# A two-layer hybrid decoder on one core: memory pieces, masks and scores of three mixers put in other places

## The reference, cut to what matters

```python
for l in range(DEPTH):
    p = rmsnorm(x, norm_mix[l]) @ w_in[l]
    y_a = hgrn2_mixer(...)             # o = state part + masked scores @ v, norm, gate
    y_b = gated_deltanet_mixer(...)    # triangular solve per 64-token chunk
    y_c = rglru_mixer(...)             # a = exp(log_a); h_t = a h_(t-1) + u, times gelu(gate)
    y_d, v_first = rwkv7_mixer(...)    # decay, delta update, group norm, bonus
    x = x + concat([y_a, y_b, y_c, y_d]) @ w_out[l]
    k, v = mem_n @ xattn_wk[l], mem_n @ xattn_wv[l]     # depends on the memory alone
    x = x + attention(rmsnorm(x, norm_xattn[l]), k, v) @ xattn_wo[l]
    x = x + (swiglu if l == 0 else moe_swiglu)(rmsnorm(x, norm_ffn[l]))
```

## Time and profile before

| | |
|---|---|
| median of 3 runs | 1963.12 us (1962.64 to 1963.27) |
| the profiled execution | 1961.31 us, of which the span of the trace is 1959.5 |
| TensorE busy, granted clock | 95% of the span, 0.981 |
| VectorE, ScalarE busy | 75%, 57% |
| layer 0: mixers | about 114 to 290 us |
| layer 1: mixers | about 667 to 845 us |
| experts | from about 957 us to the end |

### The profile page before, as it was taken

How to read it: one execution, slowest core, us unless ns; L and a number is a source line. 1 busy time by engine, 2 the same in 40 slices (tenths; PEclk the granted TensorE clock), 3 DMA queues, 4 the chain that set the end, 5 groups by cost and what they waited for, 6 DMA issues and landing times.

```text
span 1959.5 us, 29713 instructions
## 1 busy us (share of the span) xinstructions
PE 1861.4 (95%) x12520; PEld 1605.6 (82%) x12521; DVE 1465.5 (75%) x1543; ACT 1121.3 (57%) x1057; POOL 0.2 (0%) x4
## 2 busy tenths in 40 slices
PE   7997899999999978999699999999999999999996
PEld 6986789899989866897588888888888888888884
DVE  6778645554467687453789989889899898998985
ACT  5563134434344641244567777677776777767774
POOL 0000000000000000000000000000000000000000
PEclk9998999999999989999899999999999999999998
DMA  7520234355555212243599999989999999999992
GB/s 243 172 75 15 66 108 165 108 181 185 194 157 164 89 45 66 74 164 111 184 393 342 373 330 384 370 335 371 337 383 365 335 372 348 369 364 339 369 373 97
DMA packets 239450, 465.99 MB, mean 238 GB/s; under 512 B 11856, under 2 KB 87760, under 8 KB 239312
## 3 DMA queue, kind: packets, MB, share of 16 engines
q1 hardware_dynamic: 239312, 464.03, 66.4%
HBM read 462.95 MB, written 1.05 MB: 237 GB/s over the span
## 4 chain that ended last, share of the span: by engine, by line
PE 88%; DVE 9%; issue 1%; ACT 1%; DMA 1%; DVEq 0%; SPq 0%; ACTq 0%
PE ps L2148 31%; PE ps L1617 16%; PE ps L2158 16%; PE ps L1602 12%; PE ps L1637 8%; DVE MT L907 2%; PE ps L2204 2%; PE ps L2179 1%; PE ps L1682 1%; PE ps L2219 1%; DVE MT L913 1%; DVE TMP L907 1%; DVE MT L910 1%; DMA raw<-in_w_in 1%; DVE spare_hi L907 0%
## 5 line engine op out<-in xcount | busy, mean ns | idle before, releaser
L1380 DVE TENSOR_TENSOR wlo<-raw,whi 128x2048 fp32r<-128x2048 f32 x140 | 320.5, 2292 | 55.7 <-ACT whi L787 55.4
L787 ACT ACTIVATE whi<-raw 128x2048 fp32r<-128x2048 f32 x140 | 268.9, 1922 | 121.1 <-PE ps L2158 71.3
L920 DVE TENSOR_TENSOR wlo<-raw,whi 128x2048 fp32r<-128x2048 f32 x85 | 194.6, 2289 | 85.3 <-ACT whi L480 85.1
L1380 DVE TENSOR_TENSOR wlo<-PT,whi 128x2048 fp32r<-128x2048 f32 x84 | 192.1, 2293 | 31.2 <-ACT whi L787 30.1
L480 ACT ACTIVATE whi<-raw 128x2048 fp32r<-128x2048 f32 x85 | 162.1, 1907 | 64.7 <-PE ps L1637 36.6
L2148 PE MATMUL ps<-whi,hE_hi 128*128 128x512 f32 x672 | 185.5, 398 | 2.4 <-DVE hE_lo L1449 2.4
L787 ACT ACTIVATE whi<-PT 128x2048 fp32r<-128x2048 f32 x84 | 161.5, 1922 | 34.9 <-PE ps L2148 34.2
L2148 PE MATMUL ps<-wlo,hE_hi 128*128 128x512 f32 x672 | 180.2, 390 | 0.0
L2148 PE MATMUL ps<-whi,hE_lo 128*128 128x512 f32 x672 | 179.9, 390 | 0.0
L2148 PEld LDWEIGHTS ps<-wlo,hE_hi 128*128 128x128 f32 x672 | 126.2, 188 | 27.1
L2148 PEld LDWEIGHTS ps<-whi,hE_lo 128*128 128x128 f32 x672 | 126.2, 188 | 26.5
(11 more groups left out here) (297 smaller groups left out, 3356.7 us busy)
## 6 DMA issues: line engine op xcount, KB each, us to landing
raw<-in_moe_w_up SPq DMA_DIRECT2D x111, 1024.0 KB, 7.0
PT<-in_moe_w_down SPq DMA_DIRECT2D x56, 1024.0 KB, 6.5
PT<-in_moe_w_gate SPq DMA_DIRECT2D x55, 1024.0 KB, 6.9
TMP<-in_moe_w_gate SPq DMA_DIRECT2D x55, 1024.0 KB, 6.8
raw<-in_moe_w_down SPq DMA_DIRECT2D x55, 1024.0 KB, 6.1
raw<-in_w_in SPq DMA_DIRECT2D x28, 1024.0 KB, 5.3
raw<-in_ffn_w_gate SPq DMA_DIRECT2D x11, 1024.0 KB, 5.3
raw<-in_ffn_w_up SPq DMA_DIRECT2D x11, 1024.0 KB, 5.7
```

Of the source, the lines that this page charges most:

```text
L787: nc.scalar.activation(ex_hi[m % XSPL], ex_raw[m % XRAW], ACT.Copy).then_inc(S("w_hi"), 1)
L920: V.tensor_tensor(wlo[i % SPL][:, :], raw[d % RAW][:, :], whi[i % SPL][:, :].bitcast(F32), ALU.subtract).then_inc(S("w_lo"), 1)
L1380: V.tensor_tensor(ex_lo[m % XSPL], ex_raw[m % XRAW], ex_hi[m % XSPL].bitcast(F32), ALU.subtract).then_inc(S("w_lo"), 1)
```

## The change

- The third mixer's first ten operations on VectorE go from the first mixer's levels 0 to 3 into the input projection (after chunks 9 to 11), one goes from level 4 to level 6, and its end goes from the second mixer's inverse to behind the fourth's.
- The fourth mixer's decay sums go from the second mixer's inverse to the input projection; its first scaling goes from VectorE to ScalarE.
- Of the fourth mixer's scores and masks, two score products go into the second mixer's tail and two into its own inverse; one mask stands before the second mixer's output, three are in the inverse, at levels 0, 3 and 5. That inverse keeps two slices of a piece, at level 0.
- The pieces are given out anew: in layer 0 eight, eight and one slice in the first mixer, 15 and more in the second, 16 behind the fourth's inverse. Layer 1's piece 0 goes around the feed-forward's norm and piece 1 around its own first norm. The loads follow.
- The first mixer's output goes to another bank and is copied to SBUF, and bank 7 is used for pieces alone.
- The parameters are loaded by ScalarE's queue, and constants of the decays of both layers are computed before the first statistics, with two table loads more there.

The diff, cut to what is spoken of:

```diff
+PIECES = [[("xattn_wk", j) for j in range(4)] + [("xattn_wv", j) for j in range(4)],
+      [("xattn_wv", 0)] + [("xattn_wk", j) for j in range(4)] + [("xattn_wv", j) for j in range(1, 4)]]
...
+kv = [[("kv", name, layer, CM_COLS * j) for name, j in PIECES[layer]] for layer in range(DEPTH)]
...
-    pieces = [("kv", name, layer, c) for name in ("xattn_wk", "xattn_wv") for c in range(0, D, CM_COLS)]
+    if layer:
+        out += kv[1][1:2]
...
-    out += pieces[0:4] + w_out[0:1] + pieces[4:6] + w_out[1:2] + pieces[6:7] + w_out[2:4] + pieces[7:8]
+    out += kv[layer][2 * layer:4 + layer] + w_out[0:1] + kv[layer][4 + layer:6] + w_out[1:2] + kv[layer][6:7] + w_out[2:4] + kv[layer][7:8]
...
+        out += kv[1][0:1]
...
-KV_BANK = [[7, 6, 7, 7, 7, 7, 2, 1], [7, 6, 7, 7, 7, 7, 2, 3]]
+KV_BANK = [[7, 6, 7, 7, 7, 1, 2, 1], [3, 1, 7, 7, 7, 7, 2, 3]]
...
+    if l and j == 1:
+        kv_put(1, 1)
...
-            kv_put(l, 0)
...
         if v == 3:
...
-            kv_put(l, 1)
+            if l == 0:
+                kv_put(0, 0)
         if v == 4:
...
-            kv_put(l, 2)
+        if v == 6:
+            kv_put(l, 1 + l)
...
-    a(tmp(5), ps[:, 7, :], ACT.Square).then_inc(S("o_sq"), 1)
...
+    a(tmp(5), ps[:, 6, :], ACT.Square)
+    a(h_out(l), ps[:, 6, :], ACT.Copy).then_inc(S("o_sq"), 1)
+    for c in range(2):
...
+        a(K_KK[:, s_], pt(D_K)[:, s_], ACT.Copy, scale=pc("rwkv_k_k", l, c))
...
 def deltanet(l):
+    kv_put(l, 2 + l)
     rwkv_ahead(l)
...
-    kv_put(l, 3)
+    kv_put(l, 3 + l)
...
     head_rms(l)
-    kv_put(l, 4)
+    kv_put(l, 4 + l)
...
 def rwkv(l):
...
-    kv_put(l, 5)
...
+        if l == 0 and t == 0:
+            kv_put(0, 5)
...
+        if j == 0:
+            kv_put(1, 0)
...
+act.dma_start(par[:, :], A["params"]).then_inc(S("par_in"), 16)
+table("exp_and_others")
...
+for k in range(DEPTH):
...
+    a(col(lam[k], 2), par[:, o2:o2 + 2], ACT.Abs)
+    a(col(expa[k], 4), par[:, o:o + 4], ACT.Exp)
+    a(col(lam[k], 2), col(lam[k], 2), ACT.Exp, scale=-1.0)
+table("natural_log")
+for k in range(DEPTH):
+    a(col(lam[k], 2), col(lam[k], 2), ACT.Ln, bias=1.0).then_inc(S("softplus"), 1)
...
+        rglru(l, -4)
     if j == 10:
+        rglru(l, -3)
...
+    if j == 11:
+        rglru(l, -2)
...
+        ts(pt(C_X), pt(C_X), -float(np.exp(-0.5)), ALU.mult)
+        for i in range(4):
...
+            chain.link(lambda: V.tensor_tensor_scan(K_B[:, s_], ones, pt(C_X)[:, s_], 0.0, ALU.mult, ALU.add))
+        ts(col(ST_NC0, 4).unsqueeze(2), many(K_B)[:, :, HD - 1:HD], -1.0, ALU.mult)
...
-            tt(col(lam[k], 2), col(lam[k], 2), col(lam[k] + 2, 2), ALU.add)
-            ts(col(lam[k], 2), col(lam[k], 2), -16.0, ALU.mult)
 def rglru(l, v):
-    la, ex = H(7), H(13)
-    if v == 0:
+    la, ex = H(7), H(10)
+    if v == -4:
...
+        o = PCOL["lru_lambda", l][0]
+        ts(col(lam[l] + 2, 2), par[:, o:o + 2], -1.0, ALU.mult, 0.0, ALU.max)
+        tt(col(lam[l], 2), col(lam[l], 2), col(lam[l] + 2, 2), ALU.add)
+        ts(col(lam[l], 2), col(lam[l], 2), -16.0, ALU.mult)
...
-    if v == 1:
+    if v == -3:
...
-    if v == 2:
...
+    if v == -2:
+        stt(ex, ex, -1.0, la, ALU.add, ALU.mult)
     if v == 3:
-        stt(ex, ex, -1.0, la, ALU.add, ALU.mult)
...
     if v == 4:
...
+    if v == 6:
...
-            ts(K_KK[:, s_], pt(D_K)[:, s_], pc("rwkv_k_k", l, c), ALU.mult).then_inc(S("rk_kk"), 1 if c else 0)
-        for c in range(2):
...
     if v == 1:
...
-        ts(pt(C_X), pt(C_X), -float(np.exp(-0.5)), ALU.mult)
-        for i in range(4):
...
-            chain.link(lambda: V.tensor_tensor_scan(K_B[:, s_], ones, pt(C_X)[:, s_], 0.0, ALU.mult, ALU.add))
-        ts(col(ST_NC0, 4).unsqueeze(2), many(K_B)[:, :, HD - 1:HD], -1.0, ALU.mult)
...
     if v == 3:
...
 def rwkv_operands(l):
-    tt(pt(B_K), K_KK, K_EM, ALU.mult)
+    tt(pt(B_K), K_KK, K_EM, ALU.mult).then_inc(S("rk_kb"), 1)
...
+def mask(l, i, bank, dst, which):
...
+    return stt(many(dst, 8), many(ps[:, bank:bank + 2, :].rearrange("p b n -> p (b n)"), 8), 1e30, rep(which, 8),
+               ALU.min, ALU.mult)
 def deltanet(l):
...
-            head_out(l, 0, 7, tmp(0), lambda c: pc("hgrn_norm", l, c), pt(A_G), 0)
-        if v == 4:
-            rglru(l, LEVELS)
+            head_out(l, 0, h_out(l), tmp(0), lambda c: pc("hgrn_norm", l, c), pt(A_G), 0)
     inverse(2 * l, after=beside)
...
-    head_out(l, 1, 0, tmp(7), lambda c: pc("gdn_norm", l), pt(B_Z), 1)
+    mask(l, 0, 2, mt(3), strict).then_inc(S("inv_n"), 1)
+    head_out(l, 1, ps[:, 0, :], tmp(7), lambda c: pc("gdn_norm", l), pt(B_Z), 1)
 def rwkv(l):
-    for i, (bank, dst, mask) in enumerate(((2, mt(1), strict), (4, mt(2), incl), (0, mt(3), strict), (6, PT[:, 0:1024], incl))):
...
-                   ALU.min, ALU.mult)
...
-    inverse(2 * l + 1)
+    def masks(v):
+        if v == 0:
+            mask(l, 1, 4, mt(1), strict)
+        if v == 3:
+            mask(l, 2, 6, PT[:, 0:1024], incl).then_inc(S("rk_m"), 1)
+        if v == 5:
+            mask(l, 3, 6, mt(2), incl).then_inc(S("rk_m"), 1)
+    inverse(2 * l + 1, after=masks)
+    rglru(l, LEVELS)
...
+    if l and j == 3:
...
-    kv(l, 0, range(KT // 2))
+    kv(l, 2 * l, range(KT // 2))
...
         second(l, v)
-        if v == 1:
+        if v == 2:
...
-        if v == 3:
...
-        if v < 5:
-            kv(l, (v + 1) // 2, range(KT // 2) if v % 2 else range(KT // 2, KT))
+        if l and 1 <= v < 5:
+            kv(1, 2, [v + 3])
+        if l == 0 and v < 2:
+            kv(0, 0, range(5, 8) if v else [4])
+        if l == 0 and 2 <= v < 6:
+            kv(0, 1, [2 * v - 4, 2 * v - 3])
...
-    outputs_b(7, tmp(1), mt(1), h_state(l), h_qe(l)).then_inc(S("o_full"), 1)
...
+    outputs_b(6, tmp(1), mt(1), h_state(l), h_qe(l)).then_inc(S("o_full"), 1)
...
+    kv(l, 2 + l, [0])
...
     def rwkv_ahead(v):
         if v == 0:
+            kv(l, 2 + l, [1])
             head_ss(l, 0, tmp(5))
+            kv(l, 2 + l, [2, 3])
         if v == 1:
...
             mm(ps[:, 6, :], bdones, K_RN).then_inc(S("rk_ss"), 1)
+            kv(l, 2 + l, [4, 5])
+        if v == 2:
+            kv(l, 2 + l, [6, 7])
...
-            kv(l, 3, range(2 * v - 6, 2 * v - 4))
...
+            kv(l, 3 + l, range(2 * v - 6, 2 * v - 4))
     inverse(2 * l, after=rwkv_ahead)
...
     solve(6, 0, tmp(4)).then_inc(S("gd_u"), 1)
...
-    kv(l, 4, [0])
...
+    kv(l, 4 + l, [0])
...
-    kv(l, 4, [1])
+    kv(l, 4 + l, [1])
...
-    kv(l, 4, [2])
+    kv(l, 4 + l, [2])
...
     solve(6, 1, tmp(4)).then_inc(S("gd_u"), 1)
-    kv(l, 4, [3])
+    kv(l, 4 + l, [3])
...
     outputs(0, [(tmp(6), mt(2))], tmp(3)[:, 256:512], g_qe(l)).then_inc(S("o_full"), 1)
-    kv(l, 4, [4])
...
+    scores(2, pt(B_Q), pt(B_K)).then_inc(S("rk_sc"), 1)
     head_ss(l, 1, tmp(6))
-    kv(l, 4, [5])
+    scores(4, pt(A_G), pt(B_K)).then_inc(S("rk_sc"), 1)
+    kv(l, 4 + l, [4, 5])
 def rwkv(l):
...
-    scores(2, pt(A_G), pt(B_K)).then_inc(S("rk_sc"), 1)
-    scores(4, pt(A_G), pt(A_I)).then_inc(S("rk_sc"), 1)
-    kv(l, 4, [6, 7])
...
-    scores(0, pt(B_Q), pt(B_K)).then_inc(S("rk_sc"), 1)
...
-    scores(6, pt(B_Q), pt(A_I)).then_inc(S("rk_sc"), 1)
...
     def turn_operands(v):
         if v == 0:
...
-        kv(l, 5, [v, v + 1] if v == LEVELS - 1 else [v])
-        if v != 3:
-            return
-        for t in range(TT):
-            for c in range(2):
-                tr(ps[:, 6, 256 * t + P * c:256 * t + P * c + P], pt(D_V + c, 1)[:, P * t:P * t + P]).then_inc(S("rk_trv"), 1 if t and c else 0)
+            kv(l, 4 + l, [6, 7])
+        if v == 2:
...
+            scores(6, pt(B_Q), pt(A_I)).then_inc(S("rk_sc"), 1)
+        if v == 4:
...
+            scores(6, pt(A_G), pt(A_I)).then_inc(S("rk_sc"), 1)
+        if v == LEVELS - 1:
...
+            for t in range(TT):
+                for c in range(2):
+                    tr(ps[:, 6, 256 * t + P * c:256 * t + P * c + P], pt(D_V + c, 1)[:, P * t:P * t + P]).then_inc(S("rk_trv"), 1 if t and c else 0)
     inverse(2 * l + 1, after=turn_operands)
+    kv(l, 5 + l, [0, 1])
...
-    kv(l, 6, [0, 1])
...
+    kv(l, 5 + l, [2] if l else [2, 3])
...
     solve(7, 0, tmp(7)).then_inc(S("rk_u"), 1)
-    kv(l, 6, [2])
+    kv(l, 5 + l, [3] if l else [4, 5])
...
-    kv(l, 6, [3])
+    kv(l, 5 + l, [4] if l else [6, 7])
...
     right_side(1)
-    kv(l, 6, [4])
+    kv(l, 6, [5] if l else [0, 1, 2])
...
     solve(7, 1, tmp(7)).then_inc(S("rk_u"), 1)
-    kv(l, 6, [5])
+    kv(l, 6, [6] if l else [3, 4, 5])
...
     outputs(0, [(tmp(5), mt(2)), (tmp(4), PT[:, 0:1024])], tmp(3)[:, 0:256], pt(B_V)).then_inc(S("rk_o"), 1)
-    kv(l, 6, [6, 7])
+    kv(l, 6, [7] if l else [6, 7])
...
 def swiglu():
+    kv(1, 0, range(PRE))
...
     norm(3)
+    kv(1, 0, range(PRE, KT))
...
+    if l:
+        kv(1, 1, range(PRE))
     norm(norm_index(l))
+    if l:
+        kv(1, 1, range(PRE, KT))
```

(8 more changed lines are left out.)

75 lines of the change are left out of this document (36 added, 39 removed).

## The result

The changed kernel takes **1947.25 us** (median of 4 runs, 1946.15 to 1948.7), the kernel before 1963.03 (4 runs, 1962.64 to 1963.27). The ratio is 0.9924, 95% interval 0.991 to 0.9938. The forecast was 1947.8. What follows works on the traces, and the 2.7 us between them are no part of it.

What follows compares the result with a forecast made beforehand. The prediction took TensorE (88% of the chain) and VectorE (9%, mostly in two mixer stages) as the bound. Its terms, 1.4 - 8.2 - 7.2 - 7.0 + 5.4 - 1.8 + 2.1 = -15.3 us, gave 1947.8 us, range 1941 to 1953.

Steps and rivals of the forecast that it cites:

- the first mixer: VectorE's unbroken run there loses two column multiplies, one 512-column one and four two-operator ones: -4.1 us per layer.
- level 1 and level 4 of the first inverse: Second mixer's inverse: without scans level 1 gains -0.7 us, without the third mixer's end level 4 gains -2.0 us.
- layer 0's longer tail and layer 1's shorter one: Fourth mixer's tail, where TensorE never waits: six slices more in layer 0, +5.4 us; two fewer in layer 1, -1.8.
- the norms: Feed-forward's and layer 1's first norm, each now with a memory piece as at attention: +2.1 us for both.
- the start: Constants' set-up before the first statistics: +1.4 us, taking a table load as 1.28 us by the profile row, without the skill page's drain.
- the fourth mixer up to its right side: Inverse starts 4.0 us earlier, -3.6 up to level 1's product; in all -3.5 us per layer, bounds -6 to -1.5.
- Net nothing more: Fourth mixer's inverse: five levels lose a slice but get two scores and two partly hidden masks, taken as no further gain.
- (a): TensorE's clock gets better than counted: full clock is -1.4 us per fourth mixer, 1945; inside the main case, together 0.76.
- (d): Slower: thinned-out TensorE stays at half clock, 2.1 us per level; 12 levels give 25 us, 1972.6; chance 0.04.
- (c): First mixer hands its place to another wait, for exponentials or scores; half of -8.2 lost, 1951.9; chance 0.08.
- (e): Pieces buy nothing because raw buffers come late: 5 us stalls at two places, start at upper bound, 1959 to 1961; chance 0.05.
- (b): Pieces at the norms don't keep the clock: +8.7 less 1 for 2.1, total 1953.4; chance 0.07.

Runs made afterwards that it cites:

- experiment 5: Changed kernel with the third mixer's first ten operations put back into the first mixer's levels 0 to 3; 1957.35 us, ratio 0.9978 to the kernel before.
- experiment 6: Changed kernel with the third mixer's end back at level 4 of the second mixer's inverse; 1950.3 us, ratio 0.9941 to the kernel before.
- experiment 8: Kernel before with only the change's start: parameters on ScalarE's queue, both layers' decay constants before the first statistics, two more table loads; 1962.08 us, ratio 1.0002.
- experiment 2: Changed kernel with useless memory-piece slices added in the last level of the fourth mixer's inverse, real slices staying behind it; 1946.42 us, ratio 0.9928 to the kernel before.
- experiment 9: Changed kernel with the pieces of the feed-forward's and layer 1's first norm moved ahead of the last weight chunk, leaving both pauses bare; 1958.06 us, ratio 0.9982.
- Kernel 1: Changed kernel with the two slices behind the fourth mixer's inverse put into its last level; 1944.39 us, ratio 0.9911 to the kernel before.

## Why the prediction was right

**The total** was right to 0.6 us, and every stage has its sign. Part of that is luck: by the traces the stages add up to -13.3 and not -15.3, and the medians make up 2.7 us which one execution of each can't show.

**Right in mechanism and size:** the first mixer (-4.6 and -4.2 for -4.1; experiment 5), where in layer 0 a wait of 0.47 us went too; level 1 and level 4 of the first inverse (-1.0 for -0.7, -2.1 for -2.0; experiment 6); the input projection; layer 0's longer tail and layer 1's shorter one to a tenth; the norms (+2.2 for +2.1); the second inverse's start, with 3.8 us for 4.0. In the first inverse level 3 fell from 5.79 to 5.24 us too, where no change was forecast.

**Mis-sized: the start**, +1.4 forecast, +0.5 in the trace and 0 in experiment 8. The parameters are there half a microsecond sooner, and the delay of the statistics is taken up behind them. Going by the row of the table load and not by the page was right.

**Mis-sized: the fourth mixer up to its right side**, -3.5 forecast, -1.4 and -0.9 measured. The step that failed is "Net nothing more": by it nothing changes between level 1's product and the right side. By its own figures it doesn't come out either: five slices of 1.03 to 1.13 us leave, and two scores of 1.03 and the unhidden 0.85 and 1.3 of two masks come, which leaves a gain of about 1.2. For layer 0 the runs show this in its place:

| part | forecast | measured |
|---|---|---|
| start of the inverse | -4.0 | -3.77 |
| from there to level 1's product block | +0.4 | +0.69 (7.35 us for 6.66) |
| from there to the last level | 0 | -3.37 (18.99 for 22.36) |
| last level | 0 | +5.05 (9.28 for 4.23) |

So two errors of opposite sign stood in one "nothing". Up to the last level a score or a mask just takes the place of a slice (the blocks of levels 2 to 5 lie 4.4 us apart, not the 3.4 that the prediction gave as a sign), two slices go without a substitute (1.7 us), level 3 is shorter by 0.3, and level 1's block is at full clock (1.4 us, the prediction's rival (a)). In the last level three things come in. First, VectorE is late by level 5's mask, and TensorE waits 0.82 and 0.93 us for it. Second, the values' four transposes stand here now, 0.66 us; the forecast left them out, though they also leave level 3, which was 0.44 us longer than its neighbours with them. Third, the clock: from the second half's products to the right side it takes 6.18 us, and 3.54 for the same work in experiment 2, so 2.64. 1.75 + 0.66 + 2.64 is the 5.05. In layer 1 the last level is +3.77, and the inverse's first levels are 1.7 us longer than in layer 0, in part at half clock, which is why the part up to the last level gains only 0.95 us there (28.07 for 29.02).

**The rivals.** (a), a better clock, did come: the second mixer's inverse, slow at 163 to 167 us before, ran at full clock, in layer 1 too (its block of 64 took 2.08 us for 3.68), and so did the fourth's first block in layer 0. (d), a worse clock from thinner work, was right in kind: set against the best traces of the same levels it takes 2.7 and 1.4 us at the end of the fourth mixer's two inverses and another 2.7 in layer 1's two inverses ahead of that, near 7 us and not 25. (c) is out by experiment 5, (e) by the first product after each norm. (b) didn't happen, but experiment 9 shows that its premise, that the clock at a norm hangs on the piece, was not safe either.

**A faster version.** Kernel 10, the slices in the last level and useless work in layer 1's first mixer, has the lowest median, 1942.64 us; its ratio 0.99 against 0.9924 is some 4.7 us, but their intervals overlap by a hair (0.9916 and 0.991), and with more of such work the ratio was 0.992. Kernel 1 may be better than the changed one as well (0.9911). Which of the two is best isn't settled, and that either beats the changed kernel isn't shown beyond doubt.

## What to carry to other kernels

When filler is moved out of a latency-bound chain to where it fills a pause, ask of each place left behind which wait it was lying under, and look at the last step of the chain first: here it had the two waits that cost most, and the work behind it ran at the clock it left. Count every instruction that changes place, the small transposes too, and don't let a gain and a cost stand as "nothing" without adding them up. A gain of one stage in one trace is not yet a gain of the median: here nearly 4 us were taken back by the clock in stages that no edit had touched.
